# Taps of a causal convolution on TensorE, placed between the products of the projection ahead of it

## The reference

```python
def conformer_conv(h, w_pw1, b_pw1, w_dw, b_dw, ln_g, ln_b, w_pw2, b_pw2):
    u = h @ w_pw1 + b_pw1
    a, gate = jnp.split(u, 2, axis=-1)
    u = a * jax.nn.sigmoid(gate)
    u = lax.conv_general_dilated(          # causal, width 31, one filter per channel
        u, w_dw[:, None, :], window_strides=(1,), padding=[(CONV_WIDTH - 1, 0)],
        dimension_numbers=("NWC", "WIO", "NWC"), feature_group_count=CONV_CHANNELS) + b_dw
    u = jax.nn.silu(layernorm(u, ln_g, ln_b))
    return u @ w_pw2 + b_pw2
...
    bias = jnp.transpose(bias_table[t5_bucket(dist * dilation)], (2, 0, 1)).astype(jnp.float32)
```

## Time and profile before

| | us |
|---|---|
| median of 3 runs | 1901.59 |
| lowest and highest | 1899.95, 1904.19 |
| the profiled execution | 1901.71 |
| its span, from the first instruction to the last | 1899.9 |
| TensorE busy in it | 1775.3 |
| VectorE busy | 1088.5 |
| ScalarE busy | 666.1 |
| GpSimd busy | 222.3 |

### The profile page before, as it was taken

The page is one execution under the profiler, slowest core; times in us unless marked ns, Lnnn a source line. Parts: engine busy times, 40 slices in busy tenths (PEclk is TensorE's granted clock), DMA queues, the critical chain, the costliest instruction groups (busy, mean ns, idle before and its releaser), DMA issues.

```text
span 1899.9 us, 20795 instructions
## 1 busy us (share of the span) xinstructions
PE 1775.3 (93%) x7977; PEld 1394.9 (73%) x7977; DVE 1088.5 (57%) x1277; ACT 666.1 (35%) x951; POOL 222.3 (12%) x136
## 2 busy tenths in 40 slices
PE   6969699999999999999999999989899699999996
PEld 5747388888888878778888888756456478888884
DVE  6999755442444555664424444568646777626754
ACT  4234343221223244332212234555443344314431
POOL 2013210000000200010000013661200300000001
PEclk9979899999999999999999999989998899999998
DMA  4212012331232311122312322422201112322221
GB/s 178 87 44 73 1 67 89 115 117 67 88 120 91 118 67 56 68 102 107 121 67 91 116 92 100 144 73 80 68 37 67 66 67 88 124 87 88 97 92 44
DMA packets 29151, 164.54 MB, mean 87 GB/s; under 512 B 4347, under 2 KB 7035, under 8 KB 12700
## 3 DMA queue, kind: packets, MB, share of 16 engines
q1 hardware_dynamic: 24800, 158.11, 23.6%
q10 hardware_dynamic: 4284, 5.53, 0.9%
HBM read 153.92 MB, written 4.46 MB: 83 GB/s over the span
## 4 chain that ended last, share of the span: by engine, by line
PE 77%; DVE 17%; ACT 3%; issue 2%; POOL 1%; DMA 0%; ACTq 0%; DVEq 0%; SPq 0%; POOLq 0%
PE PS L592 24%; PE PS L594 24%; PE PS L593 24%; DVE CV L1662 3%; DVE T_hid L1662 3%; DVE W_lo L1632 2%; DVE R L1617 1%; DVE H_lo L1612 1%; ACT W_hi L1036 1%; DVE X L2186 1%; DVE SSUM L2075 1%; PE PS L934 1%; PE PS L886 1%; DVE CV L1675 1%; POOL ISC L1583 1%
## 5 line engine op out<-in xcount | busy, mean ns | idle before, releaser
L592 PE MATMUL PS<-H_hi,W_hi 128*128 128x512 f32 x1600 | 645.6, 403 | 42.7 <-DVE W_lo L1632 22.2
L593 PE MATMUL PS<-H_lo,W_hi 128*128 128x512 f32 x1600 | 628.7, 393 | 0.0
L594 PE MATMUL PS<-H_hi,W_lo 128*128 128x512 f32 x1600 | 628.7, 393 | 0.0
L1036 ACT ACTIVATE W_hi<-W_raw 128x2048 fp32r<-128x2048 f32 (+2 forms) x132 | 266.6, 2020 | 761.6 <-PE PS L594 761.5
L592 PEld LDWEIGHTS PS<-H_hi,W_hi 128*128 128x128 f32 x1600 | 303.8, 190 | 131.1 <-issue 56.7
L1632 DVE TENSOR_TENSOR W_lo<-W_raw,W_hi 128x2048 fp32r<-128x2048 f32 (+2 forms) x132 | 335.6, 2542 | 45.4 <-ACT W_hi L1036 45.1
L594 PEld LDWEIGHTS PS<-H_hi,W_lo 128*128 128x128 f32 x1600 | 303.6, 190 | 65.1
L593 PEld LDWEIGHTS PS<-H_lo,W_hi 128*128 128x128 f32 x1600 | 304.1, 190 | 60.3 <-issue 1.9
L592 PE MATMUL PS<-HID_hi,W_hi 128*128 128x512 f32 x640 | 250.7, 392 | 10.0 <-DVE HID_lo L1738 9.9
L1499 POOL TENSOR_TENSOR SSUM<-SSUM,SQ 128x512 f32<-128x512 f32 x52 | 93.6, 1799 | 1378.4 <-ACT SQ L1069 1375.8
L593 PE MATMUL PS<-HID_lo,W_hi 128*128 128x512 f32 x640 | 250.0, 391 | 0.0
(11 more groups left out here) (263 smaller groups left out, 1460.2 us busy)
## 6 DMA issues: line engine op xcount, KB each, us to landing
W_raw<-in_inp SPq DMA_DIRECT2D x13, 1024.0 KB, 4.8
W_raw<-in_pw SPq DMA_DIRECT2D x12, 1024.0 KB, 4.8
W_raw<-in_gu0a SPq DMA_DIRECT2D x11, 1024.0 KB, 4.7
W_raw<-in_gu0b SPq DMA_DIRECT2D x11, 1024.0 KB, 4.8
W_raw<-in_gu1a SPq DMA_DIRECT2D x11, 1024.0 KB, 4.8
W_raw<-in_gu1b SPq DMA_DIRECT2D x11, 1024.0 KB, 4.7
W_raw<-in_gu2a SPq DMA_DIRECT2D x11, 1024.0 KB, 4.7
W_raw<-in_gu2b SPq DMA_DIRECT2D x11, 1024.0 KB, 4.8
```

The costliest lines, as they stand in the source:

```text
L592: nc.tensor.matmul(dst[:], wh, x_hi[:, k, :], start=(k == first), stop=False)
L593: nc.tensor.matmul(dst[:], wh, x_lo[:, k, :], start=False, stop=False)
L594: return nc.tensor.matmul(dst[:], wl, x_hi[:, k, :], start=False, stop=(k == last))
L1036: nc.scalar.activation(W_hi[b][:, 0:n], W_raw[b][:, 0:n], ACT.Copy).then_inc(w_hi, 1)
```

## The change

- **Division of the taps.** TensorE takes all of tiles 1 and 3, 24 taps of tile 5 and 19 of tile 7 (`PE_TILES`), 105 taps. VectorE takes all of tiles 0, 2, 4 and 6, 7 taps of tile 5 and 12 of tile 7 (`DVE_TILES`), 143 taps. Between the units it does 5, 8, 21, 24, 24, 24 and 24 of them (`DVE_TAPS`; after unit 5 only 18 are ready), and four of each lot stand ahead of the weight split.
- **Place of TensorE's taps.** From the third unit on, one tap follows every k-step of a half (`FIRST_TAP` = 48 slots of 16 per unit). 80 taps lie in units 3 to 7, 25 behind them.
- **Diagonals.** They have tiles of their own (`D_hi`, `D_lo`), a ring of three chunks of six taps. ScalarE makes both parts, 12 instructions a chunk, at slots that `CHUNK_AT` gives. GpSimd makes none. The diagonal's tiles end the wait for the last product of the projection.
- **GpSimd** adds seven tiles into `SSUM`, in an order of its own, and starts when the projection is done.
- **Bias products** have four accumulators in a ring. Four stand ahead of the normalization's sums, eight behind the sums of squares; they read the table by a broadcast, and the wide copy is gone. `onehot`, `table` and `fvec` lie where `H_hi` was, and are loaded late. The wait for the scratch write moves from VectorE to ScalarE, ahead of the first new `H_hi`.
- **Start.** The root of the RMS norm comes ahead of the weight split of unit 2 on ScalarE.

```diff
+PE_TILES = [(1, 0), (3, 0), (5, 7), (7, 12)]
+PE_TAPS = [(m, t) for m, t0 in PE_TILES for t in range(t0, CONV_WIDTH)]
+PE_ENDS = [n + 1 for n, (m, t) in enumerate(PE_TAPS) if t == CONV_WIDTH - 1]
+DVE_TILES = [(0, 31), (2, 31), (4, 31), (5, 7), (6, 31), (7, 12)]
+DVE_TAPS = [5, 8, 21, 24, 24, 24, 24]
+CHUNK = 6
+CHUNKS = (len(PE_TAPS) + CHUNK - 1) // CHUNK
+FIRST_TAP = 48
+CHUNK_AT = {g: c for c, g in enumerate([33, 36, 39] + [FIRST_TAP + CHUNK * (c - 2) for c in range(3, CHUNKS)])}
+TAKE_AT = {FIRST_TAP + PE_ENDS[i] + 1: i for i in range(2)}
...
+            def conv_tap(n):
+
+                m, t = PE_TAPS[n]
+                p = [x for x, _ in PE_TILES].index(m)
+                c, x = n // CHUNK, n % CHUNK
...
+                if n in (0, *PE_ENDS):
+                    pe.wait_ge(u_lo, p + 1)
+                if x == 0:
+                    pe.wait_ge(diag_made, c + 1)
...
+                nc.tensor.matmul(AUX[p][:], d_hi, x_hi, start=n in (0, *PE_ENDS), stop=False)
+                nc.tensor.matmul(AUX[p][:], d_hi, x_lo, start=False, stop=False)
+                nc.tensor.matmul(AUX[p][:], d_lo, x_hi, start=False, stop=t == CONV_WIDTH - 1).then_inc(conv_pe, 1)
...
+            for j in range(1, L.n):
+                pe.wait_ge(w_lo, j + 1)
+                if j >= 2:
+                    pe.wait_ge(acc_free, j - 1)
+                for half in range(2):
+                    for k in range(L.kt):
+                        last = product(j % 2, L.kt, half, k, H_hi, H_lo)
+                        if k == L.kt - 1:
+                            last.then_inc(acc_ready, 1)
+                        n = SLOTS * j + 8 * half + k - FIRST_TAP
+                        if n >= 0:
+                            conv_tap(n)
+            for n in range(SLOTS * L.n - FIRST_TAP, len(PE_TAPS)):
+                conv_tap(n)
+            for h in range(4):
+                bias_product(h)
...
+            for h in range(4, ROW_HEADS):
+                bias_product(h)
+            pe.wait_ge(fvec_made, ROW_HEADS)
...
+            def diagonals(c):
+
+                if c == 0:
+                    act.wait_ge(w_parts, 2)
+                if c >= 3:
+                    act.wait_ge(conv_pe, CHUNK * (c - 2))
+                for x, (m, t) in enumerate(PE_TAPS[CHUNK * c:CHUNK * (c + 1)]):
+                    for dst, tap in ((D_hi, tap_hi), (D_lo, tap_lo)):
+                        w = tap[:, t * DT + m:t * DT + m + 1].bitcast(F32)
+                        last = nc.scalar.activation(dst[c % 3][:, x, :], ident, ACT.Copy, scale=w)
+                last.then_inc(diag_made, 1)
...
+            def beside_pw1(g):
+
+                j, s = divmod(g, SLOTS)
+                if s == 0:
+                    if j == 1:
+                        std(0)
+                        split_hi(act, L, At(0))
+                    glu_gate(j - 1)
+                    if j > 1:
+                        split_hi(act, L, At(j - 1))
+                    if j - 1 in (1, 3, 5):
+                        conv_hi((j - 2) // 2)
+                if g in CHUNK_AT:
+                    diagonals(CHUNK_AT[g])
+                if g in TAKE_AT:
+                    take_conv(TAKE_AT[g])
...
+            for h in range(4, ROW_HEADS):
+                take_bias(h)
+            act.wait_ge(fvec_made, ROW_HEADS)
+            act.dma_start(bias_scratch.rearrange("h p d -> p h d"), fvec[:]).then_inc(scr_out, 16)
...
-            for n in range(len(CONV_CHUNKS)):
-                diagonal_lo(n)
-
+            pool.wait_ge(acc_ready, 2 * (L.base + L.n))
...
             dve.wait_ge(glu_made, L.n)
-            conv_lo(2)
-            conv(3, DT)
+            conv(2, DT)
+            conv_lo(3)
+            conv(8, DT)
+            conv_joined(2)
+            conv(7, DT)
             split_lo(L, At(L.n - 1))
             conv(len(todo), DT)
+            conv_joined(3)
```

More of the change, by code:

```diff
@@ L663, in _ @@
-            linear("pw1", ready=after(h_lo_made, 0), norm=0, beside_last=bias_products)
-            pe.wait_ge(fvec_made, 12)
-            for n, (m, t0, t1) in enumerate(CONV_CHUNKS):
-                p = m - CONV_DVE + 1
-                xh, xl, row = UPS[p]
-                pe.wait_ge(diag_lo, n + 1)
-                pe.wait_ge(diag_hi, n + 1)
-                pe.wait_ge(u_lo, p + 1)
-                for t in range(t0, t1):
-                    k = TAP_CHUNK * (n % 2) + t - t0
-                    d_hi = H_hi[:, k // 4, P * (k % 4):P * (k % 4 + 1)]
-                    d_lo = H_lo[:, k // 4, P * (k % 4):P * (k % 4 + 1)]
-                    x_hi, x_lo = xh[:, row, t:t + SEQ], xl[:, row, t:t + SEQ]
-                    first, end = t == (0 if p else CONV_SPLIT), t == CONV_WIDTH - 1
-                    nc.tensor.matmul(AUX[p][:], d_hi, x_hi, start=first, stop=False)
-                    nc.tensor.matmul(AUX[p][:], d_hi, x_lo, start=False, stop=False)
-                    last = nc.tensor.matmul(AUX[p][:], d_lo, x_hi, start=False, stop=end)
-                last.then_inc(conv_pe, 1)
@@ new lines, in _ @@
+            L = layers["pw1"]
+            unit(L, At(0), H_hi, H_lo, after(h_lo_made, 0))
+            rms_sum(0)
+            for j in range(1, L.n):
[10 more added lines that the diff above has]
+                            conv_tap(n)
@@ L1140, in _ @@
[L1140 to L1151 removed]
+                nc.scalar.activation(UP_hi[:, p % 2, 0:n], U[:, m, 0:n], ACT.Copy).then_inc(u_hi, 1)
@@ new lines, in take_bias @@
+            def take_bias(h):
+                act.wait_ge(fvec_ps, h + 1)
+                nc.scalar.activation(fvec[:, h, :], (PS[2], PS[3], AUX[0], AUX[1])[h % 4][:, 0:DIAG], ACT.Copy).then_inc(fvec_made, 1)
+            for g in range(SLOTS, SLOTS * L.n):
+                beside_pw1(g)
+            glu_gate(L.n - 1)
+            conv_hi(3)
+            act.dma_start(onehot[:], a["onehot"]).then_inc(tab_in, 16)
+            act.dma_start(table[0:BUCKETS, :], a["rel_bias"]).then_inc(tab_in, 16)
@@ L1643, in _ @@
             HALO = CONV_WIDTH - 1
-            todo = [(m, t) for m in range(CONV_DVE) for t in range(CONV_WIDTH if m < CONV_DVE - 1 else CONV_SPLIT)]
+            todo = [(m, t) for m, end in DVE_TILES for t in range(end)]
+            taken_steps = [0]
             def conv(count, upto):
```

217 lines of the change are left out of this document (87 added, 130 removed).

## The result

Before: 1901.24 us median (1899.95 to 1904.19, 4 runs). After: **1875.85 us** (1874.86 to 1877.29, 4 runs); ratio 0.9865, interval 0.9848 to 0.9882. The prediction was 1879.5 us, between 1873 and 1887. The profiled execution of after took 1877.3 us, that of before 1901.7: 24.4 us less, against 22.2 foretold (by the medians 25.4 us less).

A forecast was written before the change was run, and what follows sets the result against it. The prediction took VectorE's convolution work plus GpSimd's blocking as the bound. From 1901.7 us it took 23.0 us for the convolution and added 0.8 us for the normalization, giving 1879.5 us, range 1873 to 1887 us.

The forecast's parts named there:

- What bound the kernel: Before the second projection: VectorE's string of taps, stretched by GpSimd's blocking, set the convolution's end; TensorE had room.
- GpSimd's blocking: Convolution tail: GpSimd's copy and six SSUM additions stretch VectorE's steps, 6.2 us in all; the diagonal-product stalls go.
- Slots: First projection, units 3 to 7: three products plus one tap take 1.38 us, 22.1 us per unit, without idle.
- Case C: Rival, chance 0.04: interleaving in the projection drops TensorE's clock to 1.2 GHz; 1934 us if for half the stretch.
- Convolution's end: VectorE's last convolution step ends at 188.8 us instead of 211.85, a gain of 23.0 us.
- The waits foretold at 3.8 and 0.6 us: VectorE waits for ScalarE's diagonal chunks: 3.8 us at unit 2's gate, 0.6 us at the last gate.
- TensorE's tail: Behind the projection: remaining taps and bias products until about 184.5 us, with the two sums 186.4; not the bound.
- the missing term of +2.2 us: Stretch from the convolution's end to the subtraction of the mean: no change was foretold.
- The normalization: Eight bias products behind the variance sums delay Silu and the second projection's start, a cost of 0.8 us.
- case B: Rival, chance 0.12: normalization bias products run at the lower level or wait for ScalarE's takes, costing 5.6 us; 1884 us.
- marker: VectorE's reciprocal R after the second projection; everything from there to the end was foretold to keep its length.
- case A: Rival, chance 0.13: GpSimd's additions find gaps, so TensorE's floor ends the convolution tail, 2 us earlier; 1873 to 1877 us.

The follow-up runs named there:

- Experiment 1: The kernel before with ScalarE also making the low diagonals and GpSimd none, taps left in place: 1891.27 us, ratio 0.9951.
- Experiment 5: The changed kernel with no tap between the first projection's products, all 105 TensorE taps standing behind it: 1917.13 us, ratio 1.0086.
- Experiment 4: The changed kernel with the first tap one unit later (FIRST_TAP 64), 64 taps between products instead of 80: 1871.94 us, ratio 0.9851.
- experiment 8: The changed kernel unchanged, run and profiled a second time: 1876.38 us, ratio 0.9871.
- 6: The changed kernel without the eight bias products behind the variance sums and ScalarE's takes of them: 1876.19 us, ratio 0.9876.
- experiment 3: The changed kernel with GpSimd's additions to SSUM released as each tile is made, not held until the projection's end: 1872.81 us, ratio 0.9853.
- 10: The changed kernel with FIRST_TAP 64, GpSimd's additions as tiles are made, and tile 7 cut at tap 15 instead of 12: 1874.10 us, ratio 0.9849.
- experiment 9: The changed kernel with FIRST_TAP 64 and GpSimd's additions as the tiles are made: 1876.73 us, ratio 0.9871.
- experiment 2: The changed kernel with the first four bias products moved ahead of tap 86, into TensorE's wait there: 1876.62 us, ratio 0.9873.
- 7: The changed kernel with FIRST_TAP 64, early GpSimd additions, tile 7 cut at 17, four bias products behind the mean's sums, later ScalarE takes: 1880.49 us, ratio 0.9898.
- 11: The changed kernel with all twelve bias products behind the variance sums and ScalarE's last four takes between Silu's steps: 1876.32 us, ratio 0.9865.
- 12: The changed kernel with FIRST_TAP 64, early GpSimd additions, tile 7 cut at 15, all twelve bias products behind the variance sums: 1871.24 us, ratio 0.9847.

## Why the prediction was right, and where its steps were off

**What bound the kernel: right.** The chain through VectorE and GpSimd's blocking was the thing to take away. Experiment 1 shows the blocking's share. Experiment 5 shows that without the placing the rest of the change is slower than before; its 41 us have 10 us of another cause in them, so the share of the placing as such stays open, and with it that of the new division of the taps.

**Slots: right.** 1.39 us against 1.38, no idle, clock 1.00 from 40 to 160 us. Case C did not occur: the accumulator changes every three products for 80 slots and the clock stays up. The Trainium skill, "TensorE: Matmul & The Clock Gate", section "A second HAM failure mode: psum-queue depth-cycling", tells of a kernel whose clock went up and down while it cycled through PSUM banks in each iteration; this trace shows nothing of the kind.

**Who paces whom in the projection: half seen.** The prediction compared VectorE's 20.3 to 21.7 us per unit with the slots' 22.1 and called VectorE hidden. That is right for after. It did not say that the gap in which the taps stand exists because VectorE is almost as slow, nor that the slots' 22.1 us are now the bound in units 5 to 7, where VectorE waits 0.74, 4.12 and 2.24 us. Experiment 4 took that bound away.

**Convolution's end: 188.8 foretold, 187.9 measured.** The term that was off is GpSimd's blocking, 6.2 us foretold and 5.2 measured: five instructions stretched by 0.9 to 1.1 us, while one addition fell into VectorE's wait for the last gate. The waits foretold at 3.8 and 0.6 us were 3.30 and 0.90. R came 1.8 us earlier (1.2 foretold), of which 0.7 is an earlier arrival of X and 1.1 the moved square root; but TensorE was at work on unit 2 without a wait, so only tenths of it reached the end.

**TensorE's tail: mis-sized by 4.8 us, and with it the missing term of +2.2 us.** The prediction let it end, sums included, at 186.4 us and called it no bound. It ended at 191.2: the low part of U came at 169.7 instead of 168 (GpSimd blocked it too), the taps behind that wait started at the half level (19 taps in 15.1 us instead of 13.3), and the sums behind the bias products took 3.7 us at the half level instead of 1.9. The prediction had read the earlier trace rows as if the clock stays up when there is no gap; here it fell right behind products of 33 rows. How far the tail ends behind VectorE differs between executions: with the same instructions the missing term was +2.2 us in after, +2.9 in experiment 8 and +0.4 in 6.

**The normalization: 0.8 foretold, 0.1 measured, and 0.9 in a second profile.** The mechanism is as described. Its price hangs on whether the clock falls during the eight products, which differs between executions of one kernel. The bias products took 0.68 to 0.78 us each, not 1.37 (case B did not occur); the 0.77 us that the prediction called the fastest was not.

**The sum.** Up to the second projection the forecast gain was 22.2 us and the measured one 22.4: 0.9 us more at the convolution's end, 2.2 less at the mean, 0.8 and 0.7 more behind it cancel. That they cancel is luck. The other 2.0 us of the profiled gain arise behind the marker, where the runs vary by up to 3.9 us. The time lies in case A's range, but not by its mechanism. TensorE did end last, as in case A, but at 191.2 us and not at 186.4, and not because GpSimd's additions found gaps: they cost 5.2 us.

## What to carry to other kernels

Two engines that pace each other leave gaps in the faster one, and independent work placed in those gaps costs nothing only as long as it fits: with 80 taps the last three units came every 22 us and VectorE waited, with 64 the last two came after 18.3 and 19.9 us and the last step was 6.4 us earlier. Slack is one pool: additions of GpSimd hidden in VectorE's slack and taps taken out of TensorE's units each came out 3 to 4 us faster than after alone, and together as slow as it. A wait of a few us on TensorE can cost more than itself, since what follows may run at the half level: behind the 3.22 us in after the granted clock was 0.57 over 170 to 174 us, and behind the 7.54 us in experiment 5 it was 0.50 until 87 us.

## What the runs showed of the hardware that was not expected

A bias product, which has 33 rows, is two instructions and took 0.7 us, and the granted clock could fall right behind such products without a gap. The two 128-row instructions right after the four bias products took 2.05 us in after, 2.07 in experiment 3, 1.60 in 8, 1.43 in 10 and 1.38 in 5, but 1.12 in 4, 6 and 9. Without bias products right ahead of them they took 1.02 us (before, 1, 2, 7, 11 and 12). In experiment 3 the last wait, 0.23 us, was long over, and in experiment 2 the taps right behind the four bias products stayed at the full level. The sixteen instructions of the variance sums took 7.70 us (1, 4, 6, 8), 9.21 (after, 3, 9), 9.97 (before) and up to 10.36 (5); after and 8 are one program. I did not find what decides where the clock falls.

An addition on GpSimd of 1.3 us, run while VectorE does two-input steps, waits for them as they wait for it: two additions lasted 8.13 us in experiment 9 and four lasted 6.50 in after.
